# Dealing 192 filler products differently among the steps of a recurrence on one Trainium2 core

## What is computed

```
p = h @ w_in[l]                      # r, k, v, decay and a low-rank pair, gates, merge columns
if l == 1: nu = sigmoid(v0 + (v @ v_down) @ v_up); v = v + (v_first - v) * nu
w = decay(w0 + tanh(wl) @ w_up); a = sigmoid(a0 + al @ a_up)      # the low-rank product "lora"
kk = k * k_k; kk = kk / max(||kk||, 1e-12)                       # sum over a head: "kk_sum"
S_t = S_{t-1} diag(w_t) - (S_{t-1} kk_t)(kk_t a_t)^T + v_t k_t^T;  y_t = S_t r_t
out = (groupnorm(y) + bonus) * silu(gate_c)
merged = sum over branches of sigmoid(merge gate) * (o_branch @ w_p)
```

## Time and profile before

| | |
|---|---|
| median of three runs | 2050.61 us (2049.97 to 2051.63) |
| the profiled execution | 2053.15 us, of which its span is 2051.4 us |
| mean granted TensorE clock | 0.904 of full |
| TensorE matmul / weight load / VectorE / ScalarE / GpSimd busy | 81% / 46% / 26% / 16% / 5% of the span |
| the chain that ended last | TensorE 54%, DMA 39%, VectorE 4% |

### The profile page before, as it was taken

How to read it: one execution, slowest core, us unless ns; L and a number is a source line. 1 busy time by engine, 2 the same in 40 slices (tenths; PEclk the granted TensorE clock), 3 DMA queues, 4 the chain that set the end, 5 groups by cost and what they waited for, 6 DMA issues and landing times.

```text
span 2051.4 us, 25709 instructions
## 1 busy us (share of the span) xinstructions
PE 1659.7 (81%) x11442; PEld 949.0 (46%) x11442; DVE 543.4 (26%) x1029; ACT 331.8 (16%) x721; POOL 106.5 (5%) x129
## 2 busy tenths in 40 slices
PE   6988765665767997665756659999999999999999
PEld 3544121111215862111212118778578687785785
DVE  0455010000006641100101012542433225424332
ACT  1131100000000001000000001342332013423320
POOL 0001000000000001000000000211021002110200
PEclk9998888877878998788878789999999999999999
DMA  9988999999999969999999992220533331215330
GB/s 403 376 369 316 428 427 427 428 428 427 428 427 426 388 262 386 424 428 428 427 428 428 427 412 107 101 76 28 213 144 123 134 148 59 76 32 200 144 123 21
DMA packets 44300, 588.66 MB, mean 287 GB/s; under 512 B 5024, under 2 KB 5184, under 8 KB 8224
## 3 DMA queue, kind: packets, MB, share of 16 engines
q1 hardware_dynamic: 41184, 575.05, 68.0%
q0 software_dynamic: 2576, 10.54, 1.3%
q10 hardware_dynamic: 432, 1.44, 0.2%
HBM read 585.96 MB, written 1.06 MB: 286 GB/s over the span
## 4 chain that ended last, share of the span: by engine, by line
PE 54%; DMA 39%; DVE 4%; ACT 1%; issue 1%; SPq 0%; ACTq 0%; DVEq 0%
DMA ring<-in_experts 19%; DMA arena<-in_experts 19%; PE ps L1226 17%; PE ps L1601 8%; PE ps L1492 4%; PE ps L1624 4%; PE ps L1620 4%; PE ps L1399 3%; PE ps L1977 3%; DMA ring<-in_stream 1%; PE ps L1724 1%; PE ps L1990 1%; PE ps L1190 1%; PE ps L2033 1%; PE ps L1711 1%
## 5 line engine op out<-in xcount | busy, mean ns | idle before, releaser
L1492 PE MATMUL ps<-arena 128*32 128x512 f32 x1536 | 248.4, 778 | 152.5 <-DMA arena<-in_experts 150.2
L1492 PE MATMUL ps<-ring,arena 128*32 128x512 f32 x1504 | 235.8, 758 | 147.1 <-DMA ring<-in_experts 144.0
L1226 PE MATMUL ps<-arena,ring 128*128 128x256 f32 (+1 forms) x1152 | 215.8, 350 | 4.1 <-ACT arena L726 2.5
L1226 PEld LDWEIGHTS ps<-arena,ring 128*128 128x128 f32 x1152 | 193.1, 196 | 26.0 <-ACT arena L726 3.1
L1492 PEld LDWEIGHTS ps<-arena 128*32 128x32 f32 x1536 | 49.5, 126 | 315.2 <-DMA arena<-in_experts 172.3
L1601 PE MATMUL ps<-arena,ring 128*128 128x256 f32 x768 | 189.5, 392 | 0.0
L1492 PEld LDWEIGHTS ps<-ring,arena 128*32 128x32 f32 x1504 | 47.6, 125 | 302.0 <-DMA ring<-in_experts 167.0
L1601 PEld LDWEIGHTS ps<-arena,ring 128*128 128x128 f32 x768 | 141.6, 192 | 30.3 <-issue 10.3
L2408 DVE TENSOR_TENSOR arena<-ps,gate 128x512 f32<-128x512 f32 x16 | 10.3, 685 | 308.5 <-PE ps L1492 308.5
L1620 PE MATMUL ps<-arena,ring 128*128 128x256 f32 x384 | 89.5, 382 | 0.0
L1624 PE MATMUL ps<-ring,arena 128*128 128x512 f32 x192 | 86.0, 592 | 0.0
(11 more groups left out here) (395 smaller groups left out, 1839.0 us busy)
## 6 DMA issues: line engine op xcount, KB each, us to landing
arena<-in_experts SPq DMA_DIRECT2D x96, 2048.0 KB, 35.8
ring<-in_experts SPq DMA_DIRECT2D x94, 2048.0 KB, 36.0
ring<-in_stream SPq DMA_DIRECT2D x61, 2048.0 KB, 8.6
arena<-in_stream SPq DMA_DIRECT2D x14, 2048.0 KB, 19.5
ring<-in_stream SPq DMA_DIRECT2D x2, 1696.0 KB, 7.0
arena<-in_stream SPq DMA_DIRECT2D x2, 1024.0 KB, 26.6
gate<-in_b_mod POOLq DMA_DIRECT2D x4, 512.0 KB, 11.2
ln<-in_experts SPq DMA_DIRECT2D x2, 1024.0 KB, 6.9
```

The source lines that it names most:

```text
L1226: mm = M(dst, lhs(k), rhs(k), start=k == 0, stop=k == n - 1)
L1492: mm = M(bank(b + half)[32 * e:32 * e + 32], x[:, k, 32 * e:32 * e + 32], wk(e, half), start=k == 0, stop=k == KD - 1, tile_position=(0, 3 ...
```

## The change

The table `FILL` becomes four, one for each layer and half (`FILLS`), of the same sum (192 for a layer). Two points are new: `open`, ahead of the low-rank product (in layer 1 ahead of v_down), and `down`, between v_down and v_up. The first job now goes to bank 7 instead of 6, since bank 6 still holds the low-rank columns. The wait of the low-rank product for nu is gone. `NORM_FILL` gives two of its first position to its fourth. ScalarE's order takes the two new points (its first three positions become five, all later ones shift by two).

| behind | before | (0,0) | (1,0) | (0,1) and (1,1) |
|---|---|---|---|---|
| open, down | - | 6, 0 | 4, 2 | 0, 0 |
| lora | 8 | 5 | 11 | 6 |
| kk_sum | 12 | 15 | 14 | 15 |
| rk_sum | 6 | 8 | 8 | 8 |
| tok, 5 levels | 6, 15 | 6, 15 | 6, 15 | 6, 15 |
| w1, gh, y0 | 4, 6, 6 | 2, 2, 2 | 2, 2, 2 | 2, 2, 2 |
| move1, move2, read | 5, 5, 5 | 1, 1, 2 | 1, 1, 2 | 1, 1, 2 |
| gn_mean, gn_sum | 6, 12 | 4, 27 | 4, 22 | 4, 32 |
| sum | 96 | 96 | 96 | 96 |

```diff
-FILL = {"lora": 8, "kk_sum": 12, "rk_sum": 6, "tok": 6, "level": 3, "w1": 4, "gh": 6, "y0": 6, "move1": 5, "move2": 5,
-        "read": 5, "gn_mean": 6, "gn_sum": 12}
+FILL_POINTS = ["open", "down", "lora", "kk_sum", "rk_sum", "tok"] + ["level"] * (LEVELS - 1) + [
+    "w1", "gh", "y0", "move1", "move2", "read", "gn_mean", "gn_sum"]
+FILL = dict(tok=6, level=3, w1=2, gh=2, y0=2, move1=1, move2=1, read=2, gn_mean=4)
+FILLS = {(0, 0): dict(FILL, open=6, down=0, lora=5, kk_sum=15, rk_sum=8, gn_sum=27),
+         (1, 0): dict(FILL, open=4, down=2, lora=11, kk_sum=14, rk_sum=8, gn_sum=22),
+         (0, 1): dict(FILL, open=0, down=0, lora=6, kk_sum=15, rk_sum=8, gn_sum=32)}
+FILLS[1, 1] = FILLS[0, 1]
-NORM_FILL = (6, 4, 6, 6, 4, 6, 8, 8, 16, 16, 16)
+NORM_FILL = (4, 4, 6, 8, 4, 6, 8, 8, 16, 16, 16)
...
         def fill_bank(n):
-            return 6 + n % 2
+            return 7 - n % 2
...
-                for point in range(3):
+                for point in range(5):
                     filled(point)
...
@@ second(l), TensorE
                 lora = small_t[:, 0:512]
+                filler = fill_tiles(l)
+                for _ in range(FILLS[l, 0]["open"]):
+                    next(filler)
                 if l:
...
                     project(bank(2, T)[0:32], lambda k: vdw[:, k], lambda k: s2["rkv"][:, 2, k], 4).then_inc(*Sp.up("v_down"))
+                    for _ in range(FILLS[l, 0]["down"]):
+                        next(filler)
                     pe.wait_ge(*Sa.at("v_down"))
...
                     mm.then_inc(*Sp.up("v_up"))
-                filler = fill_tiles(l)
...
                 def fill(point):
-                    for _ in range(FILL[point]):
+                    for _ in range(FILLS[K][point]):
                         next(filler)
 
                 pe.wait_ge(*S("second_act").at("tanh", l))
-                if l:
-                    pe.wait_ge(*S("second_act").at("nu", 3))
```

More of the change, by code:

```diff
@@ L52 @@
 H2 = 8
-FILL = {"lora": 8, "kk_sum": 12, "rk_sum": 6, "tok": 6, "level": 3, "w1": 4, "gh": 6, "y0": 6, "move1": 5, "move2": 5,
-        "read": 5, "gn_mean": 6, "gn_sum": 12}
-FILL_POINTS = ["lora", "kk_sum", "rk_sum", "tok"] + ["level"] * (LEVELS - 1) + ["w1", "gh", "y0", "move1", "move2", "read",
-                                                                               "gn_mean", "gn_sum"]
+FILL_POINTS = ["open", "down", "lora", "kk_sum", "rk_sum", "tok"] + ["level"] * (LEVELS - 1) + [
[5 more added lines that the diff above has]
+FILLS[1, 1] = FILLS[0, 1]
 BRANCHES = (2, 0, 1)
-NORM_FILL = (6, 4, 6, 6, 4, 6, 8, 8, 16, 16, 16)
+NORM_FILL = (4, 4, 6, 8, 4, 6, 8, 8, 16, 16, 16)
 ATT_FILL = (6, 0) + (6, 5) * 6 + (6, 6) * 2
@@ L621, in fill_bank, with filled_by @@
         def fill_bank(n):
-            return 6 + n % 2
[L624 to L629, removed]
+            return 7 - n % 2
+        def filled_by(l, p, point):
+            before = sum(FILLS[l, 0][x] for x in FILL_POINTS) if p else 0
+            return (before + sum(FILLS[l, p][x] for x in FILL_POINTS[:point + 1])) // (2 * KD)
+        for l in range(2):
+            assert filled_by(l, 1, len(FILL_POINTS) - 1) == 12
+            assert sum(FILLS[l, p][x] for p in range(2) for x in FILL_POINTS) == 12 * 2 * KD
         POINTS = len(NORM_FILL)
@@ L899, in filled @@
                 def filled(point):
-                    for n in range(filled_by(p, point - 1) if point else filled_by(p - 1, len(FILL_POINTS) - 1) if p else 0,
-                                   filled_by(p, point)):
+                    for n in range(filled_by(l, p, point - 1), filled_by(l, p, point)):
                         key, i, dst = jobs[n]
@@ L943, in recurrence @@
                       ).then_inc(*Sa.up("tok", *K, i))
-                filled(3)
+                filled(5)
                 for n in range(1, LEVELS):
@@ L949, in recurrence @@
                           ).then_inc(*Sa.up("step", *K, n, hh))
-                    filled(3 + n)
+                    filled(5 + n)
                 act.wait_ge(*Sp.at("w1", *K))
                 A(rw["wk"][:, :, :, 0:64], bank(4).rearrange("p (r h n) -> p r h n", r=4, h=2), ACT.Copy).then_inc(*Sa.up("w1", *K))
-                filled(9)
-                filled(10)
+                filled(11)
+                filled(12)
                 act.wait_ge(*Sp.at("y0", *K))
@@ L962, in recurrence @@
                 A(rw["odd"], bank(4, 256).rearrange("p (x j n) -> p x j n", x=2, j=2), ACT.Copy).then_inc(*Sa.up("odd", *K))
-                for point in range(11, 15):
+                for point in range(13, 17):
                     filled(point)
@@ L966, in recurrence @@
                 A(rw["tmp2"], rw["y"].rearrange("p j t -> p (j t)"), ACT.Square).then_inc(*Sa.up("gn_sq", *K))
-                filled(15)
+                filled(17)
                 nc.scalar.preload_act_table_set(LN_EXP)
@@ L972, in recurrence @@
                 A(rw["tmp2"], rw["tmp2"], ACT.Exp, scale=-0.5).then_inc(*Sa.up("gn_rs", *K))
-                filled(16)
+                filled(18)
             def attention_parts(l):
@@ L1759, in recurrence @@
                         mm.then_inc(*Sp.up("inv", *K, n, 1))
-                    for _ in range(FILL["level"] - 1):
+                    for _ in range(FILLS[K]["level"] - 1):
                         next(filler)
```

## The result

The changed kernel takes 2040.88 us (median of six runs, 2038.61 to 2043.21), the kernel before 2051.41 us in its six runs beside it. The ratio is 0.995, with a 95% interval of 0.9937 to 0.9962: 10.5 us or 0.5% faster. I had forecast 2036.0 us, a gain of 14.6 us, and a range of 2033.2 to 2039.6 that the median misses by 1.3 us. The direction was right, the size too large by 4.1 us, and 0.8 us more lie in the kernel before, which ran that much above its first median.

The account below looks back on a forecast made before the run. TensorE was taken to bound the second block, so only its idle time and clock count. Terms 4.0 + 4.2 + 8.2 - 0.8 - 0.2 - 0.8 = 14.6 us off the 2050.61 us median gave 2036.0 us, range 2033.2 to 2039.6.

Parts of the forecast that it names:

- Opening of layer 0: Second block, layer 0: six fills ahead of the low-rank product remove idle time and slow clock, gaining 4.0 us.
- Rival B: Both openings: the half clock comes all the same, 3.3 us given back, 2039.3 us; chance 0.12.
- kk_sum to Gram: Stretch from kk_sum to the Gram products: VectorE sets its length, more fills fit inside, gaining 8.2 us over four halves.
- Second halves: Second half of each layer: six fills instead of eight behind the low-rank product, a new 0.4 us wait, twice.
- Opening of layer 1: Second block, layer 1, v_down to kk_sum: kk_sum starts slightly earlier with 17 fills done instead of 8, gaining 4.2 us.
- Short steps: w1, gh, y0, moves, read, gn_mean: 23 fills taken from each half still leave enough cover; 0.2 us charged in all.
- Rival D: The short steps wait because their cover is too short; time up to 2075.7 us; chance 0.05.
- NORM_FILL: One 512-wide product moved from ahead of the latent transposes to ahead of the small sums: 0.4 us lost per layer.
- Rival C: The moved 512-wide product fills the wait at L1883: 0.86 us gained per layer instead of 0.4 lost, 2033.5 us; chance 0.08.
- rival E: Openings: first weights late or fills push the low-rank product out, so their 8.2 us don't come, 2044.2 us; chance 0.05.

Follow-up runs that it names:

- kk_sum and rk_sum alone: Kernel before the change with only 15 and 8 fill products behind kk_sum and rk_sum and 7 behind gn_sum in all halves: 2044.06 us, ratio 0.9958.

## Why the prediction was wrong

Its steps, one by one, against the traces:

- **Opening of layer 0**, 4.0 us: right. kk_sum came 2.7 us earlier with three more products done, at the full clock. Rival B (the clock falls all the same) did not come; the windows of both openings are at 1.00.
- **kk_sum to Gram**, 8.2 us: right, 8.9 us for the 8.6 of all four halves when tried alone. In (1,0) it was 0.2 us less than I said: 14 products leave 0.3 us of wait ahead of rk_sum and the stretch grew from 11.96 to 12.16 us. In the other three halves of the changed kernel it grew by 0.1 us (12.01 in layer 0 for 11.91).
- **Second halves**, 0.4 us lost twice: right. L1661 waits 0.23 us in the profile's rows, where I had 0.4, but the stretch takes 4.16 us, as worked out: 0.47 less than before with 0.86 us of fill less in it.
- **Opening of layer 1**, 4.2 us: 0.3 too much. v_up started at 1683.31, where I had 1690.5 less the 7.4 gained by then, 1683.1, and kk_sum lay 8.44 us behind it.
- **Short steps**, 0.2 us: right. No wait behind w1, gh, y0, the moves, read or gn_mean but for the stall inside L1853. Rival D, the one on the other side, found nothing to stand on.
- **NORM_FILL**, 0.4 us lost twice: right in sign, about 0.5 us each by the shift of the later rows, 1.4 us for both in the run that undid it. Rival C fell.

At the opening of layer 1 the changed kernel was 7.5 us ahead, and my terms gave 7.4. At the end of its first trace it was 10.3 us ahead and not 14.6. The step that failed is **what the sum put at nothing without a reason: that SyncE's weight transfers move along with the fill**. The prediction says that "the time moves only by TensorE's idle time, and by the clock", and charges idle time only where TensorE waits for an engine. It does not ask when the transfers would start; only rival E asks about weights, and only whether they would be late ("Against it: the gate weights' slot was free"). That an earlier transfer gets in the way of TensorE's instruction fetch stood in no step and no rival. The three traces of the changed kernel lost 3.4, 1.2 and 2.9 us against the one with the same order on TensorE and the transfers elsewhere, which has no stall and whose second block gained 13.7 us of the 14.6. That the transfers' place makes the stalls is shown by moving them alone; that it does so by the late instruction packets is read from the traces. Some 0.9 us remain, and they arise in layer 1, since the gain up to its opening was as forecast: the 0.3 and 0.2 above, 0.1 in its second half from kk_sum to the Gram products, 0.1 at NORM_FILL, and 0.2 at the wait L2025, which varies from trace to trace.

**The range** was too narrow for another reason. I wrote that the first block scatters by about a microsecond. But the second block began between 1224.26 and 1230.17 us in the twelve traces, and the runs of one kernel lie up to 7 us apart. The measured median is within 1.3 us of the range; a range that took this scatter in would have held it.

## What to carry to other kernels

When work is dealt out among steps, every release that rides on it moves too. For each transfer that will start earlier, ask what it will then lie beside, TensorE's instruction fetch included; steps with many short instructions are the place to keep free of large transfers. By the second block of the traces, two waits in the DMA queue were worth 1.2 to 3.4 us here. Cost a filler by its length and by the gap that ends it, and look for idle time long enough to bring the clock down behind it: 2.29 us of idle time cost 1.64 us more. A filler helps only on the side of the step from which the wait is measured: ahead of the small sums it delayed the wait, behind them it filled it.

## What was not expected of the hardware

A stall of 1 to 2 us of TensorE in the midst of a group of products, with nothing to wait for, while one weight transfer filled the DMA engines and an instruction packet of 16 KB started late within it. TensorE went on 2.2 to 2.4 us after the packet's start, nine times out of nine. The fall of the clock behind idle time came in every trace that had the idle time, but not at the same moment: with kk_sum and rk_sum alone, the low-rank product of layer 1 still ran at full speed and the fall came about 1.6 us behind its start (timeline, and the windows of one microsecond from 1688 to 1691 us).

```profile
1687.53 1.14 PE L1650 MATMUL ps<-arena,small 64*128 64x256 f32 x8 [1.75 <-ACT arena L888]
```

```profile
1688.00:1689.00 1.00, 1.00 (x9) 1.00 0.77 328
1689.00:1690.00 1.00, 1.00 (x4) 0.55 0.04 16
1690.00:1691.00 1.00, 1.00 (x4) 0.50 0.00 0
```

In the kernel before, the window from 1693 to 1694 us has 0.65, so the fall came about 0.3 us behind the start of the same product at 1692.98. kk_sum still came 6.31 us behind the low-rank product, against 6.27: the moment varies and the loss stays. The Trainium skill, page "TensorE: Matmul & The Clock Gate", section on the HAM clock gate, says that the monitor runs free of the kernel, so that the moment of a change of clock varies from run to run. The traces agree for the moment, 0.3 us in one and 1.6 us in the other.
